# Start addresses of the even K tiles' rows in both matmul operands of a two-block transformer kernel

## What is computed

```
first_block:
  z = rmsnorm(h) @ w_in              # q, k, v, three conv parts, forget logits
  y = concat(forgetting_attention(q, k, v), gate_b * short_conv(gate_c * hc))
  h = h + rmsnorm_by_group(y) @ w_out
  h = h + (silu(n @ w_gate) * (n @ w_up)) @ w_down      # n = rmsnorm(h), d_ff 5632
  x = rmsnorm(h)[:, 16:]
second_block:
  q, k, v, u, gates = split(x @ w_in)
  merged = sigmoid(g1) * (dilated_attention(q, k, v) @ w_ba) + sigmoid(g2) * (pool(u) @ w_bp)
  x = layer_norm(alpha * x + merged @ w_out)
  x = layer_norm(alpha * x + relu(x @ w_ff1)**2 @ w_ff2)   # d_ff 8192
```

## The kernel before

| layout | even high | even low | odd high | odd low |
|---|---|---|---|---|
| q stage, as read (not touched by the diff) | 64 | 1152 | 2240 | 3328 |
| `part` before | 192 | 1224 | 2256 | 3288 |

## Time and profile before

### The profile page before, as it was taken

How to read it: one execution, slowest core, us unless ns; L and a number is a source line. 1 busy time by engine, 2 the same in 40 slices (tenths; PEclk the granted TensorE clock), 3 DMA queues, 4 the chain that set the end, 5 groups by cost and what they waited for, 6 DMA issues and landing times.

```text
span 2447.8 us, 36417 instructions
## 1 busy us (share of the span) xinstructions
PE 2433.8 (99%) x14762; PEld 2173.7 (89%) x14762; DVE 1614.5 (66%) x2518; ACT 1202.2 (49%) x1728; POOL 173.9 (7%) x195
## 2 busy tenths in 40 slices
PE   8999999999999999999999999999999999999999
PEld 8999998888888888888888888888998888888887
DVE  5646676676666666667677756678885665565667
ACT  6545545544544543455555654544554443443544
POOL 0001111000000000002211102031110000000010
PEclk9999999999999999999999999999999999999999
DMA  7554456666566666665655455565566666656663
GB/s 250 180 161 139 141 165 189 200 184 194 182 198 190 189 190 189 192 190 185 197 188 167 166 185 190 184 193 186 162 196 193 189 189 189 194 190 189 183 193 117
DMA packets 125751, 449.59 MB, mean 184 GB/s; under 512 B 13840, under 2 KB 16400, under 8 KB 125584
## 3 DMA queue, kind: packets, MB, share of 16 engines
q1 hardware_dynamic: 125296, 446.91, 58.8%
q10 hardware_dynamic: 288, 0.36, 0.0%
HBM read 445.12 MB, written 2.10 MB: 183 GB/s over the span
## 4 chain that ended last, share of the span: by engine, by line
PE 96%; DVE 2%; ACT 1%; issue 0%; DMA 0%; ACTq 0%
PE out_bank L614 28%; PE out_bank L618 27%; PE out_bank L615 14%; PE out_bank L617 14%; PE out_bank L622 3%; PE out_bank L621 3%; PE out_bank L623 3%; DVE w_lo L1307 1%; ACT w_hi L895 0%; PE side_bank L734 0%; PE side_bank L694 0%; PE side_bank L749 0%; PE side_bank L725 0%; DVE h L1824 0%; DMA h<-in_tokens 0%
## 5 line engine op out<-in xcount | busy, mean ns | idle before, releaser
L1307 DVE TENSOR_TENSOR w_lo<-raw,w_hi 128x1024 fp32r<-128x1024 f32 x839 | 1037.4, 1240 | 601.0 <-ACT w_hi L895 596.9
L895 ACT CAST w_hi<-raw 128x1024 fp32r<-128x1024 f32 x840 | 878.1, 1049 | 953.6 <-PE out_bank L618 874.8
L614 PE MATMUL out_bank<-a_op,w_hi 128*128 128x512 f32 x1984 | 784.2, 395 | 0.5 <-DVE h L1334 0.3
L618 PE MATMUL out_bank<-a_op,w_hi 128*128 128x512 f32 x1984 | 776.7, 391 | 0.0
L615 PE MATMUL out_bank<-a_op,w_lo 128*128 128x256 f32 x1984 | 558.8, 282 | 0.0
L617 PE MATMUL out_bank<-a_op,w_lo 128*128 128x256 f32 x1984 | 552.0, 278 | 0.0
L617 PEld LDWEIGHTS out_bank<-a_op,w_lo 128*128 128x128 f32 x1984 | 380.1, 192 | 84.3
L615 PEld LDWEIGHTS out_bank<-a_op,w_lo 128*128 128x128 f32 x1984 | 372.9, 188 | 77.0
L614 PE MATMUL out_bank<-b_op,w_hi 128*128 128x512 f32 x992 | 389.7, 393 | 0.0
L618 PE MATMUL out_bank<-b_op,w_hi 128*128 128x512 f32 x992 | 388.0, 391 | 0.0
L614 PEld LDWEIGHTS out_bank<-a_op,w_hi 128*128 128x128 f32 x1984 | 373.1, 188 | 2.0 <-DVE w_lo L1307 0.7
(11 more groups left out here) (302 smaller groups left out, 1974.6 us busy)
## 6 DMA issues: line engine op xcount, KB each, us to landing
raw<-in_w_ff SPq DMA_DIRECT2D x256, 512.0 KB, 4.2
raw<-in_w_in SPq DMA_DIRECT2D x223, 512.0 KB, 3.7
raw<-in_w_gu SPq DMA_DIRECT2D x176, 512.0 KB, 4.2
raw<-in_w_down SPq DMA_DIRECT2D x88, 512.0 KB, 4.3
raw<-in_w_out SPq DMA_DIRECT2D x64, 512.0 KB, 4.3
raw<-in_w_ba SPq DMA_DIRECT2D x16, 512.0 KB, 3.9
raw<-in_w_bp SPq DMA_DIRECT2D x16, 512.0 KB, 3.8
out<-h SPq DMA_DIRECT2D x8, 256.0 KB, 2.3
```

Of the source, the lines that this page charges most:

```text
L614: t_.e.matmul(bank[:, :], wh, a_both, start=start, stop=False, skip_group_check=True)
L618: mm = t_.e.matmul(bank[:, :], wh, a_both, start=False, stop=stop, skip_group_check=True)
L895: a.e.copy(w_hi[:, m % SPLIT, :], raw[:, u % RAW, :]).then_inc(hi_split)
L1307: v_.e.tensor_tensor(w_lo[:, m % SPLIT, :], raw[:, u % RAW, :], w_hi[:, m % SPLIT, :].bitcast(F32), ALU.subtract).then_inc(lo_split)
```

## The change

`PLACE` becomes a pair of start words, 16 for even K tiles and 564 for odd ones. 564 is where odd rows began before (48 + 2 x 258). The even rows begin 128 bytes lower, and the distance from high to low part stays 1032 bytes. `affine_column` reaches the same two extra columns of every row by a step of 548 words instead of a reshaped view. In bytes the rows are now:

| layout | even high | even low | odd high | odd low |
|---|---|---|---|---|
| `part` after | 64 | 1096 | 2256 | 3288 |

Number, kind, shape and order of the instructions are the same on every engine.

```diff
@@ -194,7 +194,7 @@
-        ROW, PLACE = SEQ + 2, 48
+        ROW, PLACE = SEQ + 2, (16, 564)
@@ -222,7 +222,7 @@
-        last_slot = b_op[:, KT // 2 - 1, PLACE + 2 * ROW:PLACE + 4 * ROW]
+        last_slot = b_op[:, KT // 2 - 1, PLACE[1]:PLACE[1] + 2 * ROW]
@@ -239,16 +239,16 @@
         def part(op, kt, i, n=SEQ):
 
-            at = PLACE + ROW * (2 * (kt % 2) + i)
+            at = PLACE[kt % 2] + ROW * i
             return op[:, kt // 2, at:at + n]
 
         def parts(op, kt, n=SEQ):
-            at = PLACE + ROW * 2 * (kt % 2)
+            at = PLACE[kt % 2]
             return op[:, kt // 2, at:at + 2 * ROW].rearrange("p (i t) -> p i t", i=2)[:, :, 0:n]
 
         def affine_column(i, x):
-            rows = b_op[:, :, PLACE:PLACE + 4 * ROW].rearrange("p m (o i t) -> p m o i t", o=2, i=2)
-            return rows[:, :, :, i, SEQ + x]
+            at = ROW * i + SEQ + x
+            return b_op[:, :, at + PLACE[0]:at + PLACE[1] + 1:PLACE[1] - PLACE[0]]
```

## The result

| | us |
|---|---|
| before, median of 3 runs | 2450.12 |
| after, median of 3 runs | 2467.29 (2467.18 to 2467.75) |
| ratio, 95% interval | 1.0071 (1.0051 to 1.0091) |
| span in the profile, before and after | 2447.8 and 2465.4 |

The changed kernel is 17.2 us slower, and the span 17.6 us longer. That is 17.2 us above the forecast of 2450.1 us and 7.3 us above the end of the range. 20 runs of the kernel before, made beside the experiments, lie within 1.7 us of each other.

The account below looks back on a forecast made before the run. TensorE, busy 99% of the span, bounds the kernel through its matmul spacings. The profiled 2449.89 us plus 0 for writers, tables, loops and ff1 group 0, with the median 0.23 us higher, gave 2450.1 us; range 2427 to 2460 us.

Parts of the forecast that it names:

- The writers' term: ScalarE and VectorE writing the even rows: start addresses cost them nothing, and TensorE hides their waits; 0 us.
- the tables' term: Two extra columns written in the gu stage, hidden by its loops, and tables in `last_slot` that stay put: 0 us.
- ff1 group 0: 256 triples L621 to L623 reading through `part`: spacing may change some 4 ns each, 1 us either way at most; taken as 0.
- The price of a ns: Each ns added to a loop of four matmuls costs 2.85 us, since 2848 loops read through `part`.
- The loops: 2848 touched loops of L614, L615, L617, L618 at 0.693 us, 1974 us together: no change from the new addresses, 0 us.
- what one matmul saves another one gives back: Inside the loop, single durations differ between the q stage's layout and the present one, yet both add up to 1343 ns.
- a second spacing: In the q stage from 87.8 to 92.0 us, after a disturbance, same addresses: 0.700 us a loop, durations 388 to 399 ns.
- The bounds: Limits for the touched loops: 25.6 us less if each K tile kept its own cost, 19 us more at 0.700 us.
- The slower rival: Touched loops fall into a two-loop pattern 6.7 ns longer per loop: 2469 us in all, 2460 in half; chance 0.22.
- The faster rival: Even rows as in the q stage, odd as now: 7 ns less a loop, 2430 us, or 2440 at half; chance 0.30.
- The rule: Skill page on TensorE: matmul gap has no address in it, weight loads take no read bandwidth; so the change is worth 0 us.
- The estimate of 650 ns for a loop: By the skill page's formula, 1536 / 2.4 + 10 ns for the four matmuls, wherever their rows lie.

Follow-up runs that it names:

- second survey: Against the kernel before, one run with other row start bytes for most stages, ff2 getting the q stage's layout (64, 1152, 2240, 3328): 2452.90 us.
- first survey: Against the kernel before, one run with a row layout for each stage, ff1 groups 1 to 3 at 0 and 2064 bytes: 2489.0 us.

## Why the prediction was wrong

**What bounds the kernel: right.** TensorE's spacing is the span. The writers' term and the tables' term of 0 us held (408 became 407 ns, 419 stayed 419), and so did that of ff1 group 0, within 0.1 us. The price of a ns, 2.85 us, held but for 1.3 us of 19.

**The loops: the step that failed.** The prediction said of the q stage's layout: "I take this as the row nearest to the change, since one layout has the even rows of the new one and the other one has its odd rows, and both give the same loop." From this the term for the loops was put at 0 us; it measured 6.7 ns a loop, 17.7 us in all. Three things in the step were wrong. First, the q stage doesn't have the new even rows: it agrees with the new layout in the start of one row of four, and its even low row begins at 1152 bytes, not at 1096. Second, the equal loops were taken for a rule that "what one matmul saves another one gives back". The changed kernel saves 4 ns on L615 and adds 12 on the other three, and the layouts tried here go from 0.690 to 0.722 us a loop. Third, not even the q stage's own layout is sure of 0.693 us: in the second survey it takes 0.693 us in one group of ff2 and 0.700 us in the other three. The rows did hold warnings, and the text named them: each matmul depended on the addresses, and the q stage had a second spacing. The only step between spacings of the loop that they showed was 6.7 ns, and that is what the change cost.

The bounds had a flaw too. The lower one was priced by durations (9 ns less), and the prediction had itself said that durations overlap. In the changed kernel they add up to 8 ns more while the spacing grew by 6.7 ns.

**The slower rival: its size was right, its mechanism only in part.** It priced the loops at 0.700 us and the kernel at 2469 us; 0.700 and 2467.3 were measured. But it called for a pattern of two loops that a disturbance brings and another one may end, with durations that alternate within a line. The changed kernel has one value for each line, to 1 ns, and 0.700 us from the out stage to the end; no other lasting pattern was seen in it. So the 6.7 ns, taken from the second pattern of another layout, hit in part by luck. The mechanism itself does exist: with the q stage's layout it holds for three of the four ff2 groups (388 to 400 ns, 0.700 us). The range left the full slower case out, with a chance of 0.11.

**The faster rival: wrong here, and half right elsewhere.** L615 did shorten, as it said, by 4 of 7 ns. L617 and L618, of which it said that they stay at 278 and 391, went to 281 and 397, without a row of theirs moving. A K tile doesn't keep its own cost. A faster layout does exist, at 2439.9 us; in it the odd rows and the distance from high to low part have changed too.

**The rule.** The Trainium skill, page "TensorE: Matmul & The Clock Gate", section "Step-by-step: what each phase is for", has the load of the next weights take no read bandwidth from the running matmul. The prediction took from it that the change was worth 0 us, and 17.2 us were measured. The runs don't bear out a loop that is independent of where the weights lie: with no operand row moved, other addresses of the weights and of what moves with them made it 0.707 to 0.710 us instead of 0.693, and the kernel 43.2 us slower. Whether it is read bandwidth that is lost, no run here shows. The estimate of 650 ns for a loop had a weak base as well: the Trainium skill, same page, section "Back-to-back issue gap", calls that formula the gap of an isolated matmul and gives other figures for a stream of weight loads and matmuls, which this loop is.

**What stays open.** That the start addresses of the even rows cost the 17 us, inside TensorE's loops, is shown. That the place of rows and weights against each other is what counts rests on two pairs of stretches that agree and on what TensorE reads. How they act is not shown: I didn't find which reads meet, why the loops come in these steps, why one layout can hold two spacings, or a rule by which a layout's loop could be told without a run. A layout better than 0.690 us may exist.

## What to carry to other kernels

Where TensorE is the bound and its spacing is constant to a ns, start addresses of the moving rows and of the weights inside a partition are a knob of some per cent (0.690 to 0.722 us a loop here), and it can turn when a tensor ahead of them in the allocation changes size (64 bytes in a period of 256 cost 1.8% here). It can't be read off another layout: measure it, with another layout for each stage of one run, and count starts over a long stretch rather than look at durations. Read every group of a stage, because one layout showed 0.714 us in one group and 0.700 in the next, and confirm the choice with a whole run. And when two cases agree in a sum whose terms differ, ask for the reason before taking the sum as fixed.

## What the runs showed of the hardware

- The spacing of the same four matmuls, with weights loaded between, was 0.690 to 0.722 us at the 2.4 GHz level of the clock, with the start addresses as the only thing changed in them.
- Moving the weights by 128 bytes (in a period of 256) one way and all moving rows by 128 bytes the other way gave the same range of durations for each line (L614 390 to 392 ns, L615 277 to 281), which speaks for their place against each other as what counts. Moving the weights by 64 bytes, with no operand row moved, cost 43.2 us in 2450.
- One layout can have more than one lasting pattern: 0.707 and 0.710 us with the weights moved by 64 bytes, 0.714 and 0.700 us in two ff1 groups of the first survey, 0.693 and 0.700 us with the q stage's layout.
- VectorE and ScalarE wrote the rows of the down stages in the same time in every kernel here: medians of 407 to 408 ns (L1028) and 418 to 421 ns (L1538).
